# A transformer trunk: the first modulation in four feature groups, the even in-projection in a new order, 22 modulation units moved behind it

## The reference, cut to what matters

```python
def ada_modulate(c, w, b):                      # w: 2048 x 6144
    m = jax.nn.silu(c) @ w + b
    shift, scale, gate = jnp.split(m, 3, axis=-1)

shift, scale, gate = ada_modulate(c, ada_w[i, 0], ada_b[i, 0])
h = rms_norm(x, norm_g[i, 0]) * (1.0 + scale) + shift
proj = h @ w_in                                 # even mixer: 2048 x 3416
x = x + gate * mix
```

## Time and profile before

| | us |
|---|---|
| median of 3 runs (2055.79 to 2056.64) | 2056.01 |
| span of the profiled execution | 2054.0 |
| TensorE busy | 1889.3 (92%) |
| VectorE busy | 1559.5 (76%) |
| ScalarE busy | 1057.0 (51%) |
| start to the first product of the in-projection | 124.6 |
| even in-projection | 124.6 to 282.5 |
| middle stage | 282.5 to 344.0 |
| attention and out-projection of n = 0 | 344.0 to 547 |

### The profile page before, as it was taken

The page is one execution under the profiler, slowest core; times in us unless marked ns, Lnnn a source line. Parts: engine busy times, 40 slices in busy tenths (PEclk is TensorE's granted clock), DMA queues, the critical chain, the costliest instruction groups (busy, mean ns, idle before and its releaser), DMA issues.

```text
span 2054.0 us, 34033 instructions
## 1 busy us (share of the span) xinstructions
PE 1889.3 (92%) x11434; PEld 1629.2 (79%) x11434; DVE 1559.5 (76%) x2447; ACT 1057.0 (51%) x2257; POOL 220.1 (11%) x317
## 2 busy tenths in 40 slices
PE   3279998889999999999999999989999999999998
PEld 2158854766799999997877878777799999998787
DVE  4988744777778888889887888788677777778554
ACT  1145446655544545555544456565455555556443
POOL 2220001552100000000011000043000000000000
PEclk9689998999999999999999999999999999999999
DMA  8979985567588888886997886868567777765555
GB/s 325 399 278 320 339 295 170 198 229 245 200 278 281 270 273 277 278 272 231 331 332 266 271 282 203 301 220 300 193 232 224 225 234 235 224 203 177 177 189 176
DMA packets 210967, 521.25 MB, mean 254 GB/s; under 512 B 23041, under 2 KB 43010, under 8 KB 186018
## 3 DMA queue, kind: packets, MB, share of 16 engines
q1 hardware_dynamic: 180722, 316.19, 47.3%
q0 software_dynamic: 28032, 201.44, 26.9%
q10 hardware_dynamic: 2096, 2.12, 0.3%
HBM read 517.53 MB, written 2.12 MB: 253 GB/s over the span
## 4 chain that ended last, share of the span: by engine, by line
PE 73%; DVE 13%; DMA 9%; ACT 3%; issue 1%; SPq 0%; DVEq 0%; POOLq 0%; ACTq 0%
PE ps L1039 12%; PE ps L1035 12%; PE ps L1036 12%; PE ps L931 10%; PE ps L927 10%; PE ps L928 10%; DVE acc L1712 6%; DVE ring_lo L1790 3%; DMA ring<-in_od_w_in 2%; DMA first_ring<-in_ada_w 2%; DMA ring<-in_ev_w_in 1%; DMA aring<-in_ada_w 1%; PE ps L761 1%; PE ps L1131 1%; DVE L L1947 1%
## 5 line engine op out<-in xcount | busy, mean ns | idle before, releaser
L1242 ACT ACTIVATE ring_hi<-ring 128x512 fp32r<-128x512 f32 (+2 forms) x1152 | 690.8, 621 | 595.5 <-DMA ring<-in_ffn_w_up 231.6
L1790 DVE TENSOR_TENSOR ring_lo<-ring,ring_hi 128x512 fp32r<-128x512 f32 (+2 forms) x1152 | 742.3, 680 | 283.1 <-ACT ring_hi L1242 281.4
L1035 PE MATMUL ps<-hT_hi,ring_hi 128*128 128x256 f32 x2048 | 512.2, 283 | 1.5 <-PE ps L1039 0.7
L1036 PE MATMUL ps<-hT_lo,ring_hi 128*128 128x256 f32 x2048 | 507.2, 280 | 0.0
L1036 PEld LDWEIGHTS ps<-hT_lo,ring_hi 128*128 128x128 f32 x2048 | 387.3, 189 | 0.0
L1035 PEld LDWEIGHTS ps<-hT_hi,ring_hi 128*128 128x128 f32 x2048 | 384.7, 188 | 2.3 <-issue 1.2
L1039 PE MATMUL ps<-hT_hi,ring_lo 128*128 128x256 f32 x2048 | 329.2, 282 | 2.4 <-DVE ring_lo L1790 2.4
L1039 PEld LDWEIGHTS ps<-hT_hi,ring_lo 128*128 128x128 f32 x2048 | 279.2, 187 | 2.6 <-DVE ring_lo L1790 2.6
L1712 DVE SCALAR_TENSOR_TENSOR acc<-aring,cs,acc 128x2048 f32<-128x2048 f32 x112 | 263.4, 2352 | 20.6 <-DMA aring<-in_ada_w 8.8
L928 PE MATMUL ps<-ring_hi,hT_lo 128*128 128x512 f32 (+2 forms) x640 | 243.8, 382 | 0.0
L643 POOL DMA_DIRECT2D aring<-in_ada_w x176 | 94.4, 536 | 1380.7 <-DVE acc L1712 1355.6
(11 more groups left out here) (244 smaller groups left out, 1996.4 us busy)
## 6 DMA issues: line engine op xcount, KB each, us to landing
aring<-in_ada_w POOLq DMA_DIRECT2D x176, 1024.0 KB, 6.9
ring<-in_ffn_w_up SPq DMA_DIRECT2D x512, 256.0 KB, 3.0
ring<-in_ffn_w_down SPq DMA_DIRECT2D x256, 256.0 KB, 3.1
ring<-in_od_w_in SPq DMA_DIRECT2D x112, 256.0 KB, 3.5
ring<-in_ev_w_in SPq DMA_DIRECT2D x80, 256.0 KB, 5.8
first_ring<-in_ada_w POOLq DMA_DIRECT2D x16, 1024.0 KB, 7.2
ring<-in_ev_w_out SPq DMA_DIRECT2D x64, 256.0 KB, 3.5
ring<-in_od_w_out SPq DMA_DIRECT2D x64, 256.0 KB, 4.0
```

The lines of the kernel that those rows point to most:

```text
L1035: nc.tensor.matmul(o[q], hi, hT_hi[:, kt, :], start=start, stop=False, skip_group_check=True)
L1036: nc.tensor.matmul(o[q], hi, hT_lo[:, kt, :], start=False, stop=False, skip_group_check=True)
L1242: ins = nc.scalar.activation(out_, in_, f, **kw)
L1790: put(v.tensor_tensor(ring_lo[:, g, part], ring[:, g, part], ring_hi[:, g, part].bitcast(F32), ALU.subtract), lo_ok)
```

## The change

The first modulation is loaded as 16 feature tiles by four groups of 512 result columns (rows of 2 KB, four tiles in each 1 MB load) and summed group by group: 128 instructions on 128x512. TensorE turns a group's sums to columns with one product for each tile of 128 (`first_columns`, bank 6). x is turned ahead of that, unmodulated, into hT by ScalarE (`turn_first`), and hT is modulated tile by tile from SBUF (`high_first`, `first_modulation`).

The in-projection's 112 units run in the order `EV_STREAM`: blocks 0 and 1 ("front") follow the groups of features in banks 0 to 3; the other five ("back") run in chunks of 8, 4 and 4 feature tiles. A back block uses banks 4 and 5 alone and makes its products four units at a time, first all of t = 0, then all of t = 1; ScalarE copies chunk 0 to `ev`, and VectorE adds chunks 1 and 2 to it (`first_parts`, `later_parts`). Groups 2 and 3 are summed between the splits of units 16 to 79.

No unit of the following modulation stands in the in-projection any more. Of the 22, eight go to the middle stage (CMP_REST), seven to further steps of the attention, seven to heads_out (which takes all that are left). The loads of c (directly to columns), the eight bias copies and the order of the mixer's turns and units move too. The diff, cut:

```diff
-EV_ADA = (6, 11, 16, 20, 24, 28, 32, 43, 47, 51, 55, 61, 67, 71, 75, 79, 83, 87, 98, 102, 105, 108)
+GROUPS, GK = 4, KT // 4
+FRONT, BACK = (0, 1), (3, 4, 2, 5, 6)
+CHUNKS = ((0, 8), (8, 12), (12, 16))
+def even_stream():
+    front = lambda g: [(j, u) for u in range(GK * g, GK * g + GK) for j in FRONT]
+    back = lambda c: [(j, u) for j in BACK for u in range(*CHUNKS[c])]
+    return front(0) + front(1) + back(0) + front(2) + back(1) + front(3) + back(2)
...
-        if (j + 1) * 7 // 16 > j * 7 // 16:
+        if j >= 2 and (j - 1) * 7 // 14 > (j - 2) * 7 // 14:
...
-        CMP_REST = 0
+        CMP_REST = 8
         def unit_in_step(n_sub, m):
-            return m % 2 == 1 or m in (8, 16, 24) if n_sub == 0 else m % 4 != 3
+            return m % 2 == 1 or m % 4 == 0 if n_sub == 0 else m % 4 != 3
...
 gpsimd:
+            def first_loads(q):
+                g, k = q // 4, q % 4
+                for t in range(2):
+                    slot, landed_ = first_slot(q, t)
+                    if q >= 2:
+                        pool.wait_ge(ada_step.handle, 8 * (q - 1))
+                    c0 = t * D + g * NB
+                    pool.dma_start(slot.rearrange("p (k n) -> p k n", k=4),
+                                   ada_w[0, 0][4 * k * P:4 * (k + 1) * P, c0:c0 + NB]...).then_inc(landed_, 16)
+            first_loads(0)
+            first_loads(1)
             clear(-1, (0, 1))
+            for q in range(2, 4 * GROUPS):
+                first_loads(q)
...
 tensor (ahead of the flips: turn_first; even_in:)
+                def back(c, i):
+                    j, (u0, u1) = BACK[i], CHUNKS[c]
+                    for v0 in range(u0, u1, 4):
+                        for t in range(ST):
+                            if v0 == u0 and (c, i) != (0, 0):
+                                c_, i_ = (c, i - 1) if i > 0 else (c - 1, len(BACK) - 1)
+                                if c_ == 0:
+                                    pe.wait_ge(part_out.handle, 2 * i_ + t + 1)
+                                else:
+                                    pe.wait_ge(part_add.handle, 2 * len(BACK) * (c_ - 1) + 2 * i_ + t + 1)
+                            for u in range(v0, v0 + 4):
+                                p = EV_AT[j, u]
+                                ...
+                                ins = nc.tensor.matmul(o, hi, w_lo, start=False, stop=u == u1 - 1)
+                                if t == 1:
+                                    lane.done(ins, unit_used)
+                            if t == 0 and v0 + 4 == u1:
+                                lane.done(ins, part_mm)
+                for g in range(2):
+                    first_columns(g)
+                    front(g)
+                for c in range(3):
+                    for i in range(len(BACK)):
+                        if c < 2 and i == len(BACK) - 1:
+                            first_columns(c + 2)
+                        if c == 2 and i == 2:
+                            turn_blocks()
+                        back(c, i)
+                    if c < 2:
+                        front(c + 2)
...
 scalar (even_in):
+                first_back = [EV_AT[j, 0] for j in BACK]
+                for p in range(RING, len(EV_STREAM)):
+                    if p == RING:
+                        high_first(0)
+                    if p == 2 * RING:
+                        high_first(1)
+                    high("ev_in", p, w=ev_width(p))
+                    if p in (55, 87):
+                        high_first(2 + (55, 87).index(p))
+                    for i, p0 in enumerate(first_back):
+                        if p in (p0 + 11, p0 + 13):
+                            first_parts(i, (p - p0 - 11) // 2)
...
 vector:
+            def prologue():
+                sums_cleared(-1)
+                dve.wait_ge(cs_ok.handle, 1)
+                for k in range(8):
+                    first_step(0, k)
+                dve.wait_ge(prm_T.handle, 1)
+                ...                      (prm copies, rev, gs)
+                for k in range(8, 10):
+                    first_step(0, k)
+                normed(0)
+                ...                      (cbias)
+                for k in range(10, KT):
+                    first_step(0, k)
+                lows("ev_in", 0, RING)
...
 vector (even_in):
+                first_modulation(0)
+                for k in range(KT):
+                    first_step(1, k)
+                    if k % 2 == 1:
+                        low("ev_in", RING + k // 2, w=ev_width(RING + k // 2))
+                first_modulation(1)
+                steps = [(g, k) for g in (2, 3) for k in range(KT)]
+                later = {EV_AT[BACK[i], CHUNKS[c][0]]: (c, i) for c in (1, 2) for i in range(len(BACK))}
+                for p in range(2 * RING, len(EV_STREAM)):
+                    low("ev_in", p, w=ev_width(p))
+                    if p % 2 == 1 and steps:
+                        first_step(*steps.pop(0))
+                    if p in (55, 87):
+                        first_modulation(2 + (55, 87).index(p))
+                    if p == 107:
+                        flat_keys(0)
+                    if p == 109:
+                        mean_squares(0)
+                    if p == 110:
+                        flat_keys(1)
+                    if p - 7 in later:
+                        later_parts(*later[p - 7], 0)
+                    if p - 9 in later:
+                        later_parts(*later[p - 9], 1)
+                inverse(0)
+                scale_latents()
+                later_parts(2, 3, 1)
+                ...                      (keys, the last block's parts, queries)
```

More of the change, by code:

```diff
@@ new lines, in first_columns @@
+            def first_columns(g):
+                pe.wait_ge(ones_ok.handle, 1)
+                pe.wait_ge(ada_step.handle, 2 * KT * (g + 1))
+                for t in range(2):
+                    for i in range(GK):
+                        at = 2 * GK * g + GK * t + i
+                        ins = nc.tensor.matmul(ps[:, 6, at:at + 1], acc[:, t, (GK * g + i) * P:(GK * g + i + 1) * P], ones[:, 0:1],
+                                               start=True, stop=True)
+                lane.done(ins, first_cols)
@@ L1273, in _ @@
                           bass.AP(toeplitz.tensor, 0, [[1, P], [REV, SLOTS], [1, S]])).then_inc(toep_in, 16)
-            act.wait_ge(flipped.handle, 1)
-            for b in range(8):
-                run(bias_ok, bias[:, 2 * b:2 * b + 2, :], ps[:, b, :].rearrange("p (h s) -> p h s", h=2), ACT.Copy)
             def high(name, u, extra=0, w=UNIT):
@@ L1440, in attention, with head_squares, roots @@
                         exps(n)
-            def even_in():
-                def blk(j):
+            def head_squares(c0, heads, col):
+                for t in range(ST):
+                    lane.after()
+                    for h in range(heads):
+                        run(ev_sq, side[:, 3584 + h * HD:3584 + (h + 1) * HD], ev[:, t, c0 + h * HD:c0 + (h + 1) * HD], ACT.Square,
+                            scale=HD ** -0.5, accum_out=st[:, col + heads * t + h:col + heads * t + h + 1])
+            def roots(chain):
+                c0, c1 = EV_MEANS[chain]
+                act.wait_ge(ev_var.handle, chain + 1)
+                run(ev_sq, st[:, c0:c1], st[:, c0:c1], ACT.Sqrt)
@@ L1448, in blk @@
                     for t in range(ST):
-                        run(proj_out if t == 1 else None, ev[:, t, c0:c0 + n], ps[:, 2 * (j % 2) + t, 0:n], ACT.Copy)
-                def head_squares(c0, heads, col):
-                    for t in range(ST):
-                        lane.after()
-                        for h in range(heads):
-                            run(ev_sq, side[:, 3584 + h * HD:3584 + (h + 1) * HD], ev[:, t, c0 + h * HD:c0 + (h + 1) * HD], ACT.Square,
-                                scale=HD ** -0.5, accum_out=st[:, col + heads * t + h:col + heads * t + h + 1])
@@ new lines, in first_modulation @@
+            def first_modulation(g):
+                dve.wait_ge(first_cols.handle, g + 1)
+                ks, at = slice(GK * g, GK * (g + 1)), 2 * GK * g
+                put(v.tensor_copy(modc[:, 0, ks], ps[:, 6, at:at + GK]), modc_ok)
+                g0 = ROWS["norm_g"][0] + GK * g
+                put(v.scalar_tensor_tensor(modc[:, 1, ks], ps[:, 6, at + GK:at + 2 * GK], 1.0, prm[:, g0:g0 + GK], ALU.add, ALU.mult), modc_ok)
+                for b in range(2 * g, 2 * g + 2):
+                    dve.wait_ge(h_hi.handle, PAIRS_BEFORE[0, "in"] + b + 1)
+                    lane.after()
+                    for kt in (2 * b, 2 * b + 1):
+                        put(v.tensor_scalar(hT[:, kt, :], hT[:, kt, :], modc[:, 1, kt:kt + 1], modc[:, 0, kt:kt + 1], ALU.mult, ALU.add))
+                    lane.after()
+                    low_hT(PAIRS_BEFORE[0, "in"], b)
```

414 lines of the change are left out of this document (227 added, 187 removed).

## The result

| | before | after |
|---|---|---|
| median, us (4 runs each) | 2056.32 (2055.79 to 2057.24) | 2130.91 (2126.91 to 2135.23) |
| ratio | 1 | 1.0363, 95% interval 1.0339 to 1.0386 |
| span of the profiled execution | 2054.0 | 2126.4 |
| first product of the in-projection | 124.4 | 63.9 |
| the mixer's turns of k_pe (E) | 282.8 | 296.4 |

(The first product before stands at 124.4 in the trace, not at 124.6.) The change makes the kernel 74.6 us slower; 2081 was forecast, in a range of 2050 to 2106. The profiled executions differ by 72.4.

What follows compares the result with a forecast made beforehand. TensorE was taken as busy nearly everywhere except the first 124 us, held by modulation loads and sums. In-projection -9.5, middle stage +12, attention +15, heads_out +10 gave +27.5, so 2083, rounded down to 2081 us; range 2050 to 2106.

Steps and rivals of the forecast that it cites:

- at L=4.9: back(0): a weight load was taken to land 4.9 us after issue, so chunk 0 takes 63 us in place of 51.7.
- the formulas 8.2 + L and 7.0 + L: back(0): time of a wide or narrow block of eight units when the eviction loop binds, L being issue to landing.
- (a): In-projection: landings at their minimum of 2.6 us, chunk 0 takes 52, E = 257, total 2067; chance 0.12.
- if the loop did not bind: Units 16 to 79 of the in-projection: VectorE would be the next limit, 88 us for TensorE's 83.
- +11.4 for +12: Middle stage: loads of eight moved units compete with the mixer's weights, +12 us, between 0 and 21 at the outside.
- +6.4 for +15: Attention: seven moved units add 15 us, 12.8 in four steps and 2 together in three looser ones.
- A unit there costs 3.2: Attention: four steps with two units take 15.2 us, with three 18.4, so each added unit costs 3.2 us.
- +28.1 for +10: heads_out: seven moved units make 47 us of VectorE work for 37, lengthening the stage by 10, from 6 to 14.
- VectorE's idle 5 us: heads_out: VectorE idles about 5 us today, which absorbs part of the added work; the rest lengthens the stage.
- (b): In-projection: evictions never stall, E = 245, and the moved units cost all of the 37 us: 2056, no change; chance 0.08.
- (c): As (b), but the middle stage's loads slip into its pauses, costing 0 in place of 12: 2043; chance 0.13.
- (d): Queues saturate: landings of 5.7 us in chunks 0 and 1, late toeplitz chain, middle stage +21: 2104; chance 0.10.

Runs made afterwards that it cites:

- the two runs above: Changed kernel without the loads of the last eight units in heads_out: 2126.49 us; with all loads, the last eleven units' sums cut to 64 columns: 2127.41 us.

## Why the prediction was right or wrong

**The start: right in kind, and 2 to 10 us better.** First columns at 58 (66 to 72 forecast), front(0) at 64 (72), front(1) at 102.6 to 116.0 (105 to 118). The bias row did wait for the four loads ahead of it: its two parts landed 8.4 and 8.8 us after their issue, in place of 1.9, at 16.9 and 17.8 us, and the last of the four loads at 16.8. The Trainium skill, "DMA: Bandwidth & Descriptors", section "Queues, rings and completion order", has the descriptors on each DMA engine consumed in ring order, which it says of the queues of SyncE and ScalarE; for GpSimd's queue the trace agrees, with these 8.8 us. I took its bound of 24, though, and the first sum starts at 17.9. A sum of 128x512 takes 0.67 us from start to start, for the 0.63 that I took. The toeplitz load took 8.7, in its range of 8 to 15.

**back(0): the mechanism right, one term mis-sized.** The step that failed reads "at L=4.9". I took an average landing for the one that the loop waits for. With the 7.3 to 8.0 of the chain, 7.75 in the mean, the formulas 8.2 + L and 7.0 + L give 3 x 16.0 + 2 x 14.8 = 77.6; 75.9 was measured, and 75.9 to 79.0 in the kernels that share this code. The bursts' coincidence with each block could be worked out from the code, since slots and units are freed by the same stream. The loads' own part is shown: 55.3 us without them, where rival (a) had 52. Two ways of shortening the loop are shown too, the loads (20 us) and the places of the evictions (6 to 12).

**back(1) and back(2).** 45 for 35, and 35 for 33. Without these loads back(1) still takes 42, so they aren't its cause. TensorE idles for 3.9 and 3.6 us there, close to the formula, but the clock falls to 0.85 over the chunk: the sum had no term for the half clock behind a stall. It had none for VectorE either, which it named only as the next limit "if the loop did not bind" (88 us of it for 83 of TensorE). In the first half of back(1) VectorE is that limit: it is busy for 18.94 of the 20 us from 200 to 220 (the window above), and the chain that ended last runs over it alone up to the first of the two stalls:
```profile
208.62 1.03 DVE ring_lo L1957 x2
209.65 1.33 DVE acc L1861 x2
210.98 1.03 DVE ring_lo L1957 x2
212.00 1.34 DVE acc L1861 x2
```
Without the loads its work is the same and so is the stage. No run takes the sums away from this chunk, so how the 10 us divide between VectorE and the clock isn't shown.

Together E is 296.4 in place of 273: +13.6 in place of -9.5, 23 us of the error.

**The middle stage: right**, +11.4 for +12, and by contention as argued. The two parts that make it (15.4 for the units, and 4 less than before without them) were not seen, so the closeness of the number is in part luck.

**The attention: over-sized.** +6.4 for +15. Four steps do not alternate between 15.2 and 18.4 us but take 16.9 each, as three rows show (compressed logits, one in four steps; they answer):
```profile
414.79 0.18 DVE L2112 CUSTOM_DVE_ANT_0 L<-ps,cbias 128x15 f32<-128x15 f32 x1 [0.20 <-DVE rw L2124]
...
431.73 0.18 DVE L2112 CUSTOM_DVE_ANT_0 L<-ps,cbias 128x15 f32<-128x15 f32 x1 [0.17 <-DVE rw L2124]
448.65 0.18 DVE L2112 CUSTOM_DVE_ANT_0 L<-ps,cbias 128x15 f32<-128x15 f32 x1 [0.17 <-DVE rw L2124]
```
The step that failed is "A unit there costs 3.2": two such stretches with three units each take 33.9 us, where before they took 33.7 with two and three. So the 3.2 us between the two kinds of stretch were not the price of the third unit; what they are, no run shows.

**heads_out: the step that failed most in proportion**, +28.1 for +10. Two things were missing. Behind the last logits stand 19 units in place of 9, ten more and not seven, as three of the attention's fall into this stretch: 10 x 2.35 = 23.5. And I set VectorE's idle 5 us against them as if they were free; VectorE instead waits 13.7 us more for the loads, which the sum had at nothing. Taking a part of either alone away changed little, as the two runs above show.

**The first FFN: not in the sum at all.** +14.9, of which 13.8 go with a shift of the code. A reader of the diff alone can't see it; the number of instructions ahead of a loop can be counted.

**The rivals.** (a) is refuted by the 7.3 to 8.0 us, (b) and (c) by the stalls of up to 5.3 us at the evictions. (d), with L at 5.7, was the nearest at 2104; it lacked the phase, heads_out and the FFN. The direction came from terms of which two were too small and one too large. The attention's error of 9 hid part of the rest, which was 23 + 18 + 15.

## What to carry to other kernels

In a loop in which a slot's release, a load and an eviction form a ring, the sum has to use the landing of the load that lies on the chain, beside the bursts that the same loop sets off, and not the stage's median. Before work is moved into a stage, count all of it there, and check each resource against the stage's length: two limits at the same place both have to go. A stage whose code is unchanged can still move, so compare stages by marks before explaining a difference, and look at the instruction queue's packets when a loop is long.

## What the runs showed of the hardware

- A loop of TensorE of 1603 instructions, in the first FFN, costs more or less by its place in the code: the changed kernel's FFN takes 588.2 us with 37 packets of 16 KB and 574.4 with 19, and 9.1 of this lie in the loop.
- In back(0) the 256 KB loads on the chain, issued behind 2 MB of other loads, land after 7.3 to 8.0 us, where 3.5 is the median of the weights from 120 to 300 us; the 1 MB loads issued from 45 to 205 us land after 5.5 to 10.8 us (median 7.6).
- A row of 8 KB in two parts, issued on GpSimd's queue behind four 1 MB loads, lands after 8.4 and 8.8 us, right behind the last of them, in place of 1.9.
- An instruction of scale and add on 128x512 takes 0.67 us on VectorE from start to start (5.39 for eight), not the quarter of 2.35.
- Each of the four idle stretches of TensorE of 3.6 to 5.3 us in the in-projection comes with a stretch at half clock, and the windows of 20 us around them stand at 0.83.
